# Sixteen tokens of the second half taken out of a dense expert layer: rows gathered, dotted and summed beside it

## The reference

```
q      = (h @ w_q)                      # 8 heads, two halves of 128
scores = q . sub_keys                   # 128 + 128 per head
top 16 of each half, top 16 of their sums -> idx (expert number, 0 to 16383), g = softmax
ue, ve = u[idx], v[idx]                 # 8 heads x 16 = 128 experts per token, rows of 1024
act    = gelu(h . ue)
out    = sum over the 128 picks of g * act * ve
```

## Time and profile before

| | us |
| --- | --- |
| median of 3 runs | 2461.39 |
| lowest and highest | 2458.97, 2461.97 |
| span of the profiled execution | 2461.2 |
| TensorE busy in it | 2372.8 |
| VectorE, ScalarE, POOL busy | 1667.5, 1447.1, 498.6 |

### The profile page before, as it was taken

The page is one execution under the profiler, slowest core; times in us unless marked ns, Lnnn a source line. Parts: engine busy times, 40 slices in busy tenths (PEclk is TensorE's granted clock), DMA queues, the critical chain, the costliest instruction groups (busy, mean ns, idle before and its releaser), DMA issues.

```text
span 2461.2 us, 50127 instructions
## 1 busy us (share of the span) xinstructions
PE 2372.8 (96%) x16310; PEld 2175.1 (88%) x16314; DVE 1667.5 (68%) x3882; ACT 1447.1 (59%) x3296; POOL 498.6 (20%) x417
## 2 busy tenths in 40 slices
PE   8998989999999999999999989899999999999998
PEld 8997888999999878888899978889999998788887
DVE  5667775577876676666656667755778767666666
ACT  5576755555655655555555676555555556555555
POOL 0000200007767400000000003000177773000000
PEclk9999999999999999999999999999999999999999
DMA  5554465456666446566544535654566664466664
GB/s 207 191 186 142 167 246 177 152 180 187 172 188 172 137 145 222 216 210 220 198 148 171 175 134 203 213 179 154 179 184 176 187 182 109 171 221 213 219 216 162
DMA packets 165203, 449.67 MB, mean 183 GB/s; under 512 B 48060, under 2 KB 58228, under 8 KB 164852
## 3 DMA queue, kind: packets, MB, share of 16 engines
q1 hardware_dynamic: 115860, 412.44, 48.3%
q0 software_dynamic: 46080, 33.71, 6.9%
q10 hardware_dynamic: 3168, 2.39, 0.4%
HBM read 429.44 MB, written 21.66 MB: 183 GB/s over the span
## 4 chain that ended last, share of the span: by engine, by line
PE 87%; ACT 5%; DVE 5%; issue 2%; DMA 2%; ACTq 0%; POOL 0%; DVEq 0%; POOLq 0%; SPq 0%
PE bank L301 16%; PE bank L303 16%; PE bank L302 16%; PE bank L316 10%; PE bank L318 10%; PE bank L317 10%; PE bank L1613 2%; DVE w_lo L283 2%; ACT w_hi L270 2%; DMA raw<-stream 1%; ACT L343 1%; PE bank L393 1%; PE bank L1073 1%; PE bank L1595 1%; PE bank L1046 1%
## 5 line engine op out<-in xcount | busy, mean ns | idle before, releaser
L283 DVE TENSOR_TENSOR w_lo<-raw,w_hi 128x512 fp32r<-128x512 f32 x1512 | 1027.6, 690 | 718.2 <-ACT w_hi L270 704.6
L270 ACT ACTIVATE w_hi<-raw 128x512 fp32r<-128x512 f32 x1512 | 904.5, 626 | 384.7 <-PE bank L318 313.0
L301 PE MATMUL bank<-h_hi,w_hi 128*128 128x256 f32 x3360 | 963.6, 287 | 14.1 <-DVE w_lo L283 13.9
L302 PE MATMUL bank<-h_lo,w_hi 128*128 128x256 f32 x3360 | 952.5, 283 | 0.0
L303 PE MATMUL bank<-h_hi,w_lo 128*128 128x256 f32 x3360 | 952.4, 283 | 0.0
L301 PEld LDWEIGHTS bank<-h_hi,w_hi 128*128 128x128 f32 x3360 | 646.2, 192 | 25.9 <-DVE w_lo L283 18.8
L302 PEld LDWEIGHTS bank<-h_lo,w_hi 128*128 128x128 f32 x3360 | 646.8, 193 | 0.5
L303 PEld LDWEIGHTS bank<-h_hi,w_lo 128*128 128x128 f32 x3360 | 646.5, 192 | 0.0
L1204 POOL DMA_INDIRECT spread_w<-mass,cell_at x256 | 429.1, 1676 | 444.7 <-DVE mass L1491 298.0
L316 PE MATMUL bank<-w_hi,a_hi 128*128 128x512 f32 x1088 | 426.9, 392 | 10.6 <-DVE a_lo L411 5.6
L317 PE MATMUL bank<-w_lo,a_hi 128*128 128x512 f32 x1088 | 426.0, 392 | 0.0
(11 more groups left out here) (196 smaller groups left out, 1956.4 us busy)
## 6 DMA issues: line engine op xcount, KB each, us to landing
raw<-stream SPq DMA_DIRECT2D x378, 1024.0 KB
spread_w<-zeros POOLq DMA_DIRECT2D x32, 512.0 KB, 15.2
h_hi<-spread_w POOLq DMA_DIRECT2D x32, 512.0 KB, 4.8
hank<-rel_hankel SPq DMA_DIRECT2D x16, 256.0 KB, 2.6
spread_w<-mass,cell_at POOLq DMA_INDIRECT x256
rel_hankel<-rel_line SPq DMA_DIRECT2D x16, 192.0 KB
hank<-rel_hankel SPq DMA_DIRECT2D x16, 128.0 KB, 2.1
A<-subkeys SPq DMA_DIRECT2D x2, 1024.0 KB, 5.9
```

Source lines behind the costliest of these rows:

```text
L270: act.activation(w_hi[:, (ring % 2) * 2 + k, :], raw[:, slot, sub, 512 * k:512 * k + 512], ACT.Copy).then_inc(w_hi_done, 1)
L283: dve.tensor_tensor(w_lo[:, q, :], raw[:, slot, sub, 512 * k:512 * k + 512], w_hi[:, q, :].bitcast(F32), ALU.subtract).then_inc(w_parts, 1)
L301: pe.matmul(ps, hi, rhs_hi(4 * k + c), start=first, stop=False)
L302: pe.matmul(ps, hi, rhs_lo(4 * k + c), start=False, stop=False)
```

## The change

The first 16 tokens of the second half ("own") are taken out of the dense U and V and out of the one-hots.

- The two halves of the tokens change places in h: the second half has columns 0 to 127. Dense U streams columns 16 to 255 (240), A has 240 columns, and the groups of one-hots are 28 and not 32. In V the stationary tiles stay 128 columns wide; the 16 columns are zero.
- Before U, TensorE repeats the 16 tokens over the 128 partitions, 8 lanes of 16 picks for each token (two fp32 matmuls of 512 columns); VectorE multiplies by the norm's gain into h_rep.
- Behind U's block 113, ScalarE's queue issues 16 small DMAs, which bring expert numbers and weights of the 16 tokens to those lanes (lane). VectorE waits for them and works out row numbers (`lane_rows`).
- In V, POOL gathers 16 tiles of U's rows and then 16 of V's (indirect DMAs of 128 rows of 4 KB, two buffers). VectorE dots each U tile with h_rep (`row_dot`, blocks 0 to 61), ScalarE takes one gelu, VectorE weighs and sums each V tile into own (`row_add`, blocks 66 to 121). At the end TensorE sums the lanes of each token into the accumulators (two fp32 matmuls of 512 columns).
- The tile zeros has 128 columns and not 512, and is repeated 8 times and not twice in each clearing DMA.
- Weights are loaded by blocks, each as soon as its own two halves are split, and not by pairs.

```diff
-N_GROUPS = P // 4
+N_OWN = 16
+N_GROUPS = (P - N_OWN) // 4
+N_DENSE = SEQ - N_OWN
+LANE_GROUPS = P // N_OWN
+OWN_PICKS = P // LANE_GROUPS
+RING = 2
+def block_of(n):
+    j = n % OWN_PICKS
+    return 66 + j * 55 // (OWN_PICKS - 1) if n >= OWN_PICKS else j * 61 // (OWN_PICKS - 1)
...
-        zeros = sb(top, "zeros", [P, 512])
+        zeros = sb(top, "zeros", [P, 128])
...
-                sp.wait_ge(w_parts, g * 4 + 4)
-                sp.dma_start(raw[:, slot, :, :], (stream[g:g + 1] if isinstance(g, int) else stream[bass.ds(g, 1)]).rearrange("o b p c -> p (o b) c")).then_inc(raw_in[slot], 16)
+                for o in range(2):
+                    sp.wait_ge(w_parts, g * 4 + (2 * o + 2))
+                    block = stream[g:g + 1, o] if isinstance(g, int) else stream[bass.ds(g, 1), o]
+                    sp.dma_start(raw[:, slot, o, :], one(block)).then_inc(raw_in[2 * slot + o], 16)
...
-                    pool.dma_start(spread_w[layer][8 * i:8 * i + 8].rearrange("e (a b) t -> (e a) (b t)", a=16).rearrange("p (n f) -> p n f", f=512),
-                                   spread(zeros[:].rearrange("p (n f) -> p n f", n=1), 1, 2)).then_inc(cleared.sem, 16)
+                    pool.dma_start(spread_w[layer][8 * i:8 * i + 8].rearrange("e (a b) t -> (e a) (b t)", a=16).rearrange("p (n f) -> p n f", f=128),
+                                   spread(zeros[:].rearrange("p (n f) -> p n f", n=1), 1, 8)).then_inc(cleared.sem, 16)
...
-            A = sb(part, "A", [P, KEYS, SEQ])
+            A = sb(part, "A", [P, KEYS, N_DENSE])
+            row = sb(part, "row", [P, RING, D])
+            h_rep = sb(part, "h_rep", [P, D])
...
+                def fetch_row(n):
+                    i, values = n % RING, n // OWN_PICKS
+                    if n >= RING:
+                        pool.wait_ge(row_used.sem, row_used.base + n - RING + 1)
+                    pool.indirect_dma_start(row[:, i, :], None, stream_rows if values else u_rows,
+                                            bass.IndirectOffsetOnAxis(ap=lane_at[:, values, n % OWN_PICKS:n % OWN_PICKS + 1], axis=0)).then_inc(row_in[i].sem, 16)
...
+                pool.wait_ge(lanes_done.sem, lanes_done.base + 1)
+                pool.wait_ge(rep_done.sem, rep_done.base + 1)
+                for n in range(RING):
+                    fetch_row(n)
                 pool.wait_ge(scattered.sem, scattered.base + 16 * P)
...
                 act.wait_ge(routed.sem, routed.base + 1)
+                for g in range(LANE_GROUPS):
+                    for i, kept in enumerate((own_at, picks[:, 2, :])):
+                        act.dma_start(lane[N_OWN * g:N_OWN * g + N_OWN, i, :], kept[0:N_OWN, OWN_PICKS * g:OWN_PICKS * g + OWN_PICKS]).then_inc(lanes_in.sem, 16)
                 plain(FREE, 4)
...
+                dve.tensor_scalar(turn_own, consts[:, C_REP:C_REP + P], rstd[:, 1:2], None, ALU.mult).then_inc(rep_scaled.sem, 1)
+                dve.memset(a_hi[:, :, 0:N_OWN].bitcast(F32), 0.0)
+                dve.memset(a_lo[:, :, 0:N_OWN].bitcast(F32), 0.0)
...
+                def lane_rows():
+                    dve.wait_ge(lanes_in.sem, lanes_in.base + 2 * LANE_GROUPS * 16)
+                    code = lane[:, 0, :]
+                    num, key = first_of, dots[:]
+                    ch(dve.tensor_copy(num, code))
+                    dve.tensor_scalar(lane_at[:, 0, :], code, float(layer * KEYS * KEYS), None, ALU.add)
+                    ch(dve.tensor_scalar(num, num, 7, None, ALU.logical_shift_right))
+                    ch(dve.tensor_copy(key, num))
+                    ch(dve.tensor_scalar(code, code, float(KEYS), float(first_row_v(layer)), ALU.mult, ALU.add))
+                    dve.scalar_tensor_tensor(out=lane_at[:, 1, :], in0=key, scalar=float(1 - KEYS * KEYS), in1=code, op0=ALU.mult, op1=ALU.add).then_inc(lanes_done.sem, 1)
...
+                def row_dot(j):
+                    wait_row(j)
+                    row_j = row[:, j % RING, :]
+                    dve.scalar_tensor_tensor(out=row_j, in0=row_j, scalar=1.0, in1=h_rep[:], op0=ALU.mult, op1=ALU.mult, accum_out=dots[:, j:j + 1]).then_inc(row_used.sem, 1)
+                def row_add(j):
+                    n = OWN_PICKS + j
+                    wait_row(n)
+                    if j:
+                        dve.wait_ge(row_used.sem, row_used.base + n)
+                    dve.scalar_tensor_tensor(out=own, in0=row[:, n % RING, :], scalar=dots[:, j:j + 1], in1=own, op0=ALU.mult, op1=ALU.add).then_inc(row_used.sem, 1)
...
+                for k in range(N_V - 1):
+                    if k % 8 == 3 and k < 120:
+                        spread_product((k + 5) // 8)
+                    split_lo(dve, B_V + k + 1, (k + 1) % 4)
+                    part_lo(dve, src, k + 1, (k + 1) % 2, N_DENSE)
+                    if k == block_of(OWN_PICKS):
+                        dve.wait_ge(own_gelu.sem, own_gelu.base + 1)
+                        ch(dve.tensor_tensor(dots[:], dots[:], lane[:, 1, :], ALU.mult))
+                    for j in range(OWN_PICKS):
+                        if k == block_of(j):
+                            row_dot(j)
+                        if k == block_of(OWN_PICKS + j):
+                            row_add(j)
...
-                blocks_loop(pe, B_U, FREE, body)
+                pe.wait_ge(rep_scaled.sem, rep_scaled.base + 1)
+                pe.wait_ge(sc_read.sem, sc_read.base + 4)
+                for k in range(2):
+                    ins = pe.matmul(bank[4 + k][:, :], turn_own, x[:, 1, 512 * k:512 * k + 512], start=True, stop=True)
+                ins.then_inc(rep_mm.sem, 1)
+                blocks_loop(pe, B_U, FREE, up_dense)
                 pe.wait_ge(routed.sem, routed.base + 1)
+                pe.wait_ge(rep_done.sem, rep_done.base + 1)
...
+                pe.wait_ge(row_used.sem, row_used.base + 2 * OWN_PICKS)
+                for k in range(2):
+                    pe.matmul(bank[6 + k][:, :], turn_own, own[:, 512 * k:512 * k + 512], start=False, stop=False)
+                down_last(pe, PEER_BLOCKS - 1, (PEER_BLOCKS - 1) % 4, N_V - 1, bank[4:8], PEER_COLS)
```

More of the change, by code:

```diff
@@ L265, in split_hi_half @@
             slot, sub = ring // 2, ring % 2
-            if sub == 0 and k == 0:
-                act.wait_ge(raw_in[slot], blk * 4 + (16 - 4 * ring))
+            if k == 0:
+                act.wait_ge(raw_in[ring], blk * 4 + (16 - 4 * ring))
             act.wait_ge(w_used, blk * 2 + (k + 1))
@@ L318, in down_part, with down_block @@
             return pe.matmul(ps, lo, w_hi[:, q, :], start=False, stop=last)
[L320 removed]
+        def down_block(pe, b, ring, k_blk, acc, first, cols):
             blk = b + place.first
@@ L1169, in trunk @@
             best_f = sb(part, "best_f", [P, TOPK])
-            whole = sb(part, "whole", [P, P], I32)
             diag_peer = picks[:, 0:2, :]
-            g_all = hot[:].rearrange("p a b c d -> p (a b c d)")[:, 0:D]
+            g_all, own = [hot[:].rearrange("p a b c d -> p (a b c d)")[:, D * i:D * i + D] for i in range(2)]
+            turn_own = picks[:, 2, :]
+            own_at = turned[:, 0:2, :].rearrange("p a b -> p (a b)").bitcast(F32)
+            first_of = best_at[:].rearrange("p a b c -> p (a b c)")[:, 0:OWN_PICKS].bitcast(I32)
+            whole = feats[:, 0:2, :].rearrange("p a b -> p (a b)").bitcast(I32)
             lists = hot[:, 0, :, 0:2, :]
@@ L1212, in peer_gpsimd @@
                 fetch(1)
-                for i in range(2, 16):
+                i = 2
+                for n in range(RING, 2 * OWN_PICKS):
+                    if i < 16 and 8 * i - 21 <= block_of(n - RING):
+                        pool.wait_ge(spread_done.sem, spread_done.base + i - 1)
+                        fetch(i)
+                        i += 1
+                    fetch_row(n)
+                for i in range(i, 16):
                     pool.wait_ge(spread_done.sem, spread_done.base + i - 1)
@@ L1219, in peer_sync @@
                 sp.dma_start(keys_t, subkeys[layer]).then_inc(keys_in.sem, 16)
+                sp.dma_start(row[:, 0, :], spread(ffn_g[layer:layer + 1], 0, P)).then_inc(gain_row_in.sem, 16)
                 if layer + 1 < DEPTH:
@@ L1355, in peer_scalar, with eights @@
                 act.wait_ge(g_read.sem, g_read.base + N_GROUPS)
[L1356 removed]
+                part_hi(act, src, 0, 0, N_DENSE)
                 def ahead(k, blk, ring, n, i):
                     split_hi(act, blk + 1, (ring + 1) % 4)
[L1360 to L1365 removed]
+                    part_hi(act, src, k + 1, (ring + 1) % 2, N_DENSE)
+                def eights(first, end):
+                    with act.Fori(0, end - first) as n:
+                        for i in range(8):
+                            if i == 7:
+                                act.wait_ge(spread_done.sem, n + (spread_done.base + first + 2))
+                            ahead(n * 8 + (8 * first + i), n * 8 + (B_V + 8 * first + i), i % 4, n, i)
+                eights(0, 8)
```

(9 more changed lines are left out.)

144 lines of the change are left out of this document (78 added, 66 removed).

## The result

The changed kernel takes 2469.1 us (median of five runs, 2467.9 to 2473.7) against 2461.4 (2459.0 to 2464.3) for the kernel before: 7.7 us or 0.3% more by the medians. The ratio taken over all the runs is 1.0043, with a 95% interval of 1.003 to 1.0056. It is slower by 0.3 to 0.4%, where I had forecast 0.5% faster. The time lies within the range, but the sign is wrong.

What follows compares the result with a forecast made beforehand. TensorE's stream was taken as the bound (busy 96%). 2461.2 - 41.0 - 11.0 + 19.6 + 3.4 + 1 + 15 gave 2448 us, 0.5% faster; own range 2436 to 2460, some 0.85 of chance from 2420 to 2491.

Steps and rivals of the forecast that it cites:

- zeros of 128 columns: POOL's clearing DMAs in the mixer: 1024 short elements each make issues longer and delay the power; +15 us, both layers.
- The 2 to 3 us that I expected back in layer 0: Mixer, layer 0: TensorE's loss to late weights soon after the clears would be regained, leaving +8 us there.
- POOL in proportion: Rival for the clearing DMAs: issue cost proportional to elements, +46 in place of +15, 2479 us; chance 0.12.
- clearing over 40 us: Sign on POOL's queue in the mixer that the forecast is wrong; it expected 30 us from first record to end.
- The lane DMAs: Behind U's block 113: 16 issues at 0.45 us on ScalarE and VectorE's wait stall TensorE; +19.6 us, both layers.
- U with 240 columns: Dense U: 6144 matmuls stream 16 columns less, 0.1133 us each instead of 0.120; -41.0 us.
- The rival in which the load sets 0.120 us: Dense U: weight loads, not the stream, set the pace, so narrowing gains nothing; 2489 us, chance 0.25.
- Four groups of one-hots: One-hot stage on VectorE between U and V: four groups fewer at 1.37 us in two layers; -11.0 us.
- The repeated rows: Between scores and U: two fp32 matmuls, 1.7 us, fit into TensorE's idle time there; 0.
- The own matmuls: End of V: two fp32 matmuls of 512 columns with nothing beside them, 1.7 us a layer; +3.4 us.
- The rows in V: V: gathered rows dotted and summed on VectorE lose some tenths where they meet spread products; +1 us in all.
- Single blocks: Weights loaded by single blocks on SP's queue, refilled earlier; -3 to 0 us, taken as 0.

Runs made afterwards that it cites:

- before_z128: Kernel before with only the zeros tile cut to 128 columns, so each clearing DMA has 1024 runs of 512 B: 2498.3 us, ratio 1.0153.
- both2: Changed kernel with POOL's power ahead of the clears, lane DMAs spread over eight U blocks, ScalarE's wait for them removed, row numbers at block 127: 2409.9 us, ratio 0.9801.

## Why the prediction was wrong, step by step

**zeros of 128 columns: +37 us, not +15.** This is the step that failed. The place and the mechanism were right: clears, power, VectorE, w_lo, TensorE. The size was wrong, because I drew a line through the issues of 128 and 256 runs and put 1.5 ns on each run. The two issues were also not alike: the 128 runs go from DRAM to SBUF, the 256 from SBUF to DRAM. Issues of 1024 runs take 0.84 us at the least, of 512 runs 0.71, of 256 0.72: 0.16 ns a run from 256 to 1024, a tenth of that. In place of the long issue came a cause that I had not thought of: POOL stops for 14 and 11 us, each time until all the DMAs that it has issued have landed. The power ended 8 us later than forecast in each layer, and the lower clock, which this term had left out, added 1.3 and 2.0 us. Of the 2 to 3 us that I expected back in layer 0, 1.9 came: the wait before 332.13 is gone, in before_z128 as well. My bounds (0 to +46) held the value, and the rival nearest to it, POOL in proportion, gave 2479 for another reason. The sign of failure that I had named, clearing over 40 us, was set too high: it took 39.3 us in layer 0 (296.17 to 335.48). With +37 in place of +15 the sum is 2470. That this meets the measured 2469.1 is in part luck: the errors in U (-5.7) and in the lanes (+5.4) cancel.

The rule that I had weighed against this term, "emit a lot of descriptors before the incremental cost shows up" (the Trainium skill, DMA: Bandwidth & Descriptors, section Anatomy of one DMA), agrees with the trace as to the issue: 0.84 us against 0.72 for four times the runs. As to the queue it does not help: the 14 us stop is no part of it.

**The lane DMAs: about +25 us, not +19.6** (the 22 us that both2 took off, and what its two stretches of 240 matmuls still have over 240 x 0.1117 = 26.8 us, 1.3 and 2.2). Each link held but one. From ScalarE's first issue to TensorE's next matmul I had 10.8 us and it was 13.65 (788.24 to 801.89). Landing, row numbers and w_lo came out as worked out; an issue took 0.64 us from start to start, and I had 0.45 from SyncE's queue. 15 steps x 0.19 = 2.8 us a layer, nearly all of the 6 us that the stage is off by. The 1.5 us for the clock were 1.4 in layer 0 and 2.4 in layer 1.

**U with 240 columns: 46.7 us, not 41.0.** The rival in which the load sets 0.120 us fell by its result, but its premise is half true. A floor that does not depend on the columns does bound U, at 0.1117 us and already at 240 columns, and the plain fp32 pairs speak for the weight load as its cause. The 0.120 us at 256 columns are not that bound. The slope that I took from 256 and 512 columns gives 0.1133 at 240 and 0.1167 at 248; measured were 0.1117 and 0.1144, 1.6 and 2.3 ns less. The Trainium skill (TensorE: Matmul & The Clock Gate, section LDWEIGHTS) gives 107 ns for this load, an estimate by its formula; the measured floor is 5 ns above.

**Four groups of one-hots: -11.3 us**, forecast -11.0.

**The repeated rows: 0, as forecast** (by the stages; no run prices them alone). The scores' stage is 1.4 us longer in each layer (+2.8), and the wait of 1.55 us in U's block 1 is gone; that part is in U's -43.3. **The own matmuls: +3.4**, as forecast. The timeline of V's end:

```profile
1228.47 0.39 PE L337 MATMUL bank<-w_hi,a_lo 128*128 128x512 f32 x1
1228.70 1.88 PE L1757 MATMUL bank<-hot,picks 128*128 128x512 f32 x4
1230.01 0.79 PE L335 MATMUL bank<-w_hi,a_hi 128*128 128x512 f32 x1
1230.64 0.40 PE L336 MATMUL bank<-w_lo,a_hi 128*128 128x512 f32 x1
```

From 1228.70 to 1230.64 it is 1.94 us where one matmul has 0.23: 1.7.

**The rows in V: +2 us, not +1.** VectorE's work rose from 203.86 to 229.64 us in the stretch of 300, and TensorE lost time in two places of a layer only. They are the ones in which a row meets a spread product. First the stretch (columns as above), then the first of the two places in the timelines of VectorE and TensorE:

```profile
900.00:1200.00 300.00, 299.26 (x1319) 247.16 (x1318) 229.64 (x387) 171.34 (x331) 39.96 (x40) 1.00 0.79 264
```

```profile
1063.42 1.28 DVE L1675 SCALAR_TENSOR_TENSOR hot<-row,dots,hot 128x1024 f32<-128x1024 f32 x1
1064.62 1.22 DVE L1658 TENSOR_TENSOR A<-A,h_hi 128x1024 f32<-128x1024 f32 x1
1065.75 1.28 DVE L302 TENSOR_TENSOR w_lo<-raw,w_hi 128x512 fp32r<-128x512 f32 x2
...
1067.50 0.49 PE L335 MATMUL bank<-w_hi,a_hi 128*128 128x512 f32 x1 [0.47 <-DVE a_lo L434]
```

The steps of TensorE there are 0.86 and 0.65 us where 0.23 is usual: 1.05 us a layer. No row came late, and the DMA share of 0.79 (0.74 forecast) did no harm.

**Single blocks: 0**, forecast 0.

**The sum.** -46.7 - 11.3 + 37 + 25 + 3.4 + 2 gives +9 to +10, where +7.7 was measured; the terms are good to 1 or 2 us each, and what is left is not assigned. Short stretches of lower clock lie elsewhere from one kernel to the next: V is 350.8 us in layer 0 and 349.5 in layer 1 of the kernel before, and its first 14 and first 7 matmuls ran at the lower clock (0.43 us from start to start and not 0.23). In the changed kernel only the first 7 of layer 1 did. At one clock the V stage's +3.8 would be some +6.6, so the rows in V may cost nearer to 3 us than 2.

## What to carry to other kernels

Where a change cuts a DMA of POOL's queue into more and shorter pieces, count the pieces that it issues in one batch and not only the length of an issue: here the queue stopped the engine for 11 to 22 us, until all that it had issued had landed, and with it everything behind it on that engine. Read the length of such a stop from the landings in the trace before. Put what others wait for ahead of such a batch; here two moved lines were worth 37 us. Price an issue from the queue on which it will stand, together with the waits that follow it there: 0.64 us on ScalarE, where SyncE's neighbouring rows said 0.45.

## What the runs showed of the hardware that I had not expected

- POOL stopped issuing DMAs after 7168 runs (7 DMAs of 1024) and after 7680 (15 of 512), each time where one more would have made 8192, and never with 4096 (16 of 256). DMAs of the batch that had landed by then made no room. All 38 stops, of 11 to 22 us, ended 0.39 to 0.52 us after the DMA issued last had landed, and then up to seven of 1024 runs went out again.
- An fp32r matmul with a fresh 128-column weight load starts every 0.1117 us at 224 and at 240 columns, every 0.1144 at 248 and every 0.1200 at 256. From 248 to 256 that is 0.70 ns a column, more than the 0.417 ns that lie between 256 and 512 (0.1067 us in 256 columns). Why is open.
- While TensorE stood for 10.6 to 19.5 us its granted clock fell to 0.50, and it stayed so for 14 to 26 matmuls more: 1.3 to 2.4 us lost behind a stand.
